# Routing and gathering the tokens of a mixture-of-experts layer tile by tile, and moving one gated product into the first group of experts

## The reference

```python
merged = sigmoid(ga) * (a @ w_br_a) + sigmoid(gb) * (o @ w_br_b)
x = layernorm(DN_ALPHA * x + merged @ w_out, ln1_g, ln1_b)
moe_out = hier_moe(x, w_rg, w_re, w1, w3, w2)
ple_term = sigmoid(x @ w_ple_gate) * (ple @ w_ple)
x = layernorm(DN_ALPHA * x + moe_out + ple_term, ln2_g, ln2_b)

def hier_moe(x, w_rg, w_re, w1, w3, w2):      # cut: shapes left out
    g_top, g_idx = top_k(softmax(x @ w_rg), 1)            # one of 4 groups
    e_logits = (x @ w_re) of that group                   # 8 experts in a group
    e_top, e_idx = top_k(softmax(e_logits), 2)            # two of them
    wts = g_top * e_top / e_top.sum()
    # each token goes to its two experts e: (silu(x @ w1[e]) * (x @ w3[e])) @ w2[e]
    # and the two results are added with the weights wts
```

## Time and profile before

| | us |
|---|---|
| median of 3 runs (lowest, highest) | 1733.82 (1733.11, 1735.64) |
| the profiled execution | 1733.89 |
| its span in the trace | 1732.1 |
| TensorE busy in it | 1411.0 (81%) |
| VectorE busy in it | 468.5 (27%) |
| ScalarE busy in it | 280.3 (16%) |

### The profile page before, as it was taken

How to read it: one execution, slowest core, us unless ns; L and a number is a source line. 1 busy time by engine, 2 the same in 40 slices (tenths; PEclk the granted TensorE clock), 3 DMA queues, 4 the chain that set the end, 5 groups by cost and what they waited for, 6 DMA issues and landing times.

```text
span 1732.1 us, 20248 instructions
## 1 busy us (share of the span) xinstructions
PE 1411.0 (81%) x8536; PEld 651.8 (38%) x8537; DVE 468.5 (27%) x1025; ACT 280.3 (16%) x677; POOL 49.5 (3%) x95
## 2 busy tenths in 40 slices
PE   5999999999977667766597999989999577667753
PEld 3556665553422212221254566645433122212211
DVE  3132563452211011100224415634512111011004
ACT  1322232111100000000125323230201000000001
POOL 1200000000000000000021000000000000000000
PEclk9999999999988878888798999999999888888887
DMA  8312413667999999999842024147499999999992
GB/s 281 106 47 98 152 50 114 230 283 295 426 427 426 427 427 426 427 425 427 346 151 74 1 98 152 49 141 297 190 404 426 427 427 427 427 426 426 427 427 102
DMA packets 97454, 490.98 MB, mean 283 GB/s; under 512 B 9264, under 2 KB 15184, under 8 KB 47696
## 3 DMA queue, kind: packets, MB, share of 16 engines
q1 hardware_dynamic: 92608, 478.16, 67.6%
q0 software_dynamic: 4752, 11.45, 2.0%
HBM read 486.69 MB, written 2.89 MB: 283 GB/s over the span
## 4 chain that ended last, share of the span: by engine, by line
PE 55%; DMA 29%; SPq 10%; DVE 3%; ACT 2%; issue 1%; DVEq 0%; POOL 0%; ACTq 0%
PE bank L862 52%; SPq L721 10%; DMA arena<-in_w_e_up 6%; DMA arena<-in_w_e_down 6%; DMA lb<-in_w_e_down 5%; DMA cst<-in_w_e_gate 3%; PE bank L900 2%; DMA xT<-in_w_e_gate 2%; DMA arena<-in_w_e_gate 2%; DMA cst<-in_w_e_up 2%; DMA lb<-in_w_e_gate 2%; DMA xT<-in_w_e_down 1%; DMA ring<-in_w_in 1%; DVE x_sb L1769 0%; DVE arena L1766 0%
## 5 line engine op out<-in xcount | busy, mean ns | idle before, releaser
L862 PE MATMUL bank<-ring,arena 128*32 128x512 f32 (+4 forms) x1720 | 458.0, 628 | 184.3 <-DMA arena<-in_w_e_up 41.1
L862 PE MATMUL bank<-arena 128*32 128x512 f32 (+11 forms) x2648 | 537.0, 540 | 68.1 <-DMA cst<-in_w_e_gate 22.2
L862 PE MATMUL bank<-ring,xT 128*32 128x128 f32 (+5 forms) x2496 | 451.8, 390 | 4.7 <-ACT xT L1436 2.3
L862 PEld LDWEIGHTS bank<-ring,arena 128*32 128x32 f32 (+1 forms) x1720 | 136.3, 135 | 460.6 <-issue 451.3
L862 PEld LDWEIGHTS bank<-ring,xT 128*32 128x32 f32 (+1 forms) x2496 | 218.0, 140 | 207.6 <-issue 189.5
L862 PEld LDWEIGHTS bank<-arena 128*32 128x32 f32 (+5 forms) x2648 | 203.8, 144 | 216.4 <-issue 211.1
L862 PE MATMUL bank<-cst,arena 128*32 128x512 f32 (+2 forms) x240 | 124.6, 659 | 1.7 <-ACT arena L1687 1.7
L862 PE MATMUL bank<-x_sb,arena 128*128 128x512 f32 (+1 forms) x192 | 95.7, 624 | 0.6 <-DVE arena L2192 0.6
L862 PE MATMUL bank<-lb,arena 128*32 128x512 f32 x160 | 91.2, 724 | 0.0
L2172 DVE TENSOR_TENSOR arena<-arena,bank 128x512 f32<-128x512 f32 x16 | 11.0, 688 | 272.7 <-PE bank L862 272.7
L862 PE MATMUL bank<-xT,arena 128*32 128x512 f32 x128 | 76.0, 750 | 0.0
(11 more groups left out here) (226 smaller groups left out, 894.3 us busy)
## 6 DMA issues: line engine op xcount, KB each, us to landing
arena<-in_w_e_gate SPq DMA_DIRECT2D x64, 1024.0 KB, 26.2
arena<-in_w_e_up SPq DMA_DIRECT2D x60, 1024.0 KB, 26.5
arena<-in_w_e_down SPq DMA_DIRECT2D x58, 1024.0 KB, 26.3
ring<-in_w_e_down SPq DMA_DIRECT2D x52, 1024.0 KB, 26.4
ring<-in_w_e_up SPq DMA_DIRECT2D x48, 1024.0 KB, 26.8
ring<-in_w_e_gate SPq DMA_DIRECT2D x44, 1024.0 KB, 26.6
ring<-in_w_in SPq DMA_DIRECT2D x32, 1024.0 KB, 9.5
ring<-in_w_out SPq DMA_DIRECT2D x8, 1024.0 KB, 7.2
```

The costliest lines, as they stand in the source:

```text
L862: return pe.matmul(out, lhsT, rhs, start=first, stop=last, skip_group_check=True)
```

## The change

- Ranks are counted in the order 2, 0, 1 and tile by tile (`rank`): those of tiles 2 and 0 while tile 1 is still being mixed. `tri` has 512 on its diagonal, so a routed token's rank comes out as 512 and more, and `places` (512 to 543) takes the role of the counting row. The two steps that turned ranks to positions are gone, and the selection compares with the bank itself (`place_tile`).
- `gather_first` multiplies `x` as the stationary side with `sel`, 128 columns at a time, and so writes the first quad's tokens already transposed, for tiles 2 and 0 before tile 1's transposes and for tile 1 after its ranks. `X0`, its copies and the eight transposes are gone.
- `route_tile` has fewer steps: the logits of the experts are masked straight from the bank by one `min`, and the second one-hot is added in one step.
- The statistics of the norm are taken for each half of `w_out`'s product when it is added. Tile 1 is normalised in halves, and its first transposes wait for the first half (`x_half`). `w_out`'s columns are put in the order of `x` on the host.
- `plain(0, 0)` moves from ahead of quad 0 to behind `Y` of quad 0, and the transposed choice `ST0` behind `plain(0, 1)`. The slots of `pg`'s first half are given out later in `expert_slots`.

TensorE before, in layer 0, from the product of half of tile 0's large gate matrix (`ring,xT`) to the first expert product. `arena,cst` are rank and count matmuls, `x_sb,arena` the gathers.

The diff, cut to its core:

```diff
+RANK0 = 512
...
-            (("wo", 0, 1), 6), (("rt", 2), 7), (("t1", 0, 0), 0), (("t1", 0, 1), 1), (("rt", 0), 3), (("wo", 1, 1), 2),
...
+            (("rt", 2), 7), (("t1", 0, 0), 0), (("t1", 0, 1), 1), (("wo", 0, 1), 6), (("rt", 0), 3),
...
-    j += [(("Y", 0), 5), (("Y", 1), 6)] + plain(1, 1, 1, 2) + plain(1, 2, 3, 4) + combine
+    j += [(("Y", 0), 5), (("Y", 1), 6)] + plain(0, 0, 7, 0) + plain(1, 1, 1, 2) + plain(1, 2, 3, 4) + combine
...
     first_g, first_y = 3, 7
-    turns += [(first_g + 1.5, i) for i in pg[0:2]] + [(first_y + 1.5, i) for i in [pl] + pg[2:4] + [XT_SLOT]]
+    turns += [(first_y + 1.2, i) for i in pg[0:2]] + [(first_y + 1.5, i) for i in [pl] + pg[2:4] + [XT_SLOT]]
 
...
-                    for h in range(2):
-                        job_read(pe, (layer, "t1", t, h))
                     b = open_bank((layer, "rt", t))
                     for c in range(8):
+                        if c % 4 == 0:
+                            job_read(pe, (layer, "t1", t, c // 4))
...
                     for h in range(2):
+                        if t == 1 and h == 0:
+                            pe.wait_ge(x_half, layer + 1)
+                        else:
+                            pe.wait_ge(ln_out, ln_place(2 * layer + 1, t))
                         transposes(layer, ("t1", t, h), [((c % 4) * P, P, x[0:NT[t], t, c * P:c * P + P]) for c in range(4 * h, 4 * h + 4)])
...
+                def rank(t):
+
+                    pe.wait_ge(route_out, 3 * layer + MIX_ORDER.index(t) + 1)
+                    b = open_bank((layer, "rk", t))
+                    for k, s in enumerate(MIX_ORDER[0:MIX_ORDER.index(t)]):
+                        mm(b[0:NT[t], 0:32], ones[0:NT[s], 0:NT[t]], route[0:NT[s], s, :], k == 0, False)
+                    done(mm(b[0:NT[t], 0:32], tri[0:NT[t], 0:NT[t]], route[0:NT[t], t, :], t == MIX_ORDER[0], True))
+
+                def gather_first(tiles):
+
+                    for h in range(2):
+                        key = (layer, "XT0", h)
+                        b = open_bank(key) if tiles[0] == MIX_ORDER[0] else bank(key)
+                        for t in tiles:
+                            for c in range(4):
+                                k = 4 * h + c
+                                ins = mm(b[:, c * P:(c + 1) * P], x[0:NT[t], t, k * P:k * P + P], sel[0:NT[t], t, :],
+                                         t == MIX_ORDER[0] and c == 0, t == MIX_ORDER[2])
+                        if tiles[-1] == MIX_ORDER[2]:
+                            done(ins)
+
                 turn_mixed(2)
-                mix(0, 1)
+                half_mix(0, 0)
                 pe.wait_ge(rows_in, 80 * (layer + 1))
                 router(2)
                 turn_mixed(0)
-                half_mix = lambda h: project_half(layer, ("wo", 1), 1, mT, [("wo", 1, 0), ("wo", 1, 1)], h)
-                half_mix(0)
+                half_mix(0, 1)
                 router(0)
-                half_mix(1)
+                half_mix(1, 0)
+                rank(2)
+                rank(0)
+                half_mix(1, 1)
+                pe.wait_ge(sel_early, layer + 1)
+                gather_first((2, 0))
+                turn_mixed(1)
+                router(1)
...
-                turn_mixed(1)
-                router(1)
-                half_gate = lambda h: project_half(layer, ("pg", 0), 0, xT, [("pg", 0, 0), ("pg", 0, 1)], h)
-                half_gate(0)
-
-                pe.wait_ge(route_out, 3 * (layer + 1))
-                for t in range(3):
-                    b = open_bank((layer, "rk", t))
-                    for s in range(t):
-                        mm(b[0:NT[t], 0:32], ones[:, 0:NT[t]], route[:, s, :], s == 0, False)
-                    done(mm(b[0:NT[t], 0:32], tri[0:NT[t], 0:NT[t]], route[0:NT[t], t, :], t == 0, True))
+                rank(1)
+                pe.wait_ge(sel_out, QUADS * layer + 1)
+                gather_first((1,))
                 b = open_bank((layer, "cnt"))
...
-                pe.wait_ge(sel_out, QUADS * layer + 1)
-                gather([(layer, "X0", h) for h in range(2)])
-                pe.wait_ge(selw_out, QUADS * layer + 1)
-                transpose_choice((layer, "ST0"))
-                turn_tokens([(layer, "X0", h) for h in range(2)], [(layer, "XT0", h) for h in range(2)])
...
                         plain(0, 1)
+                        pe.wait_ge(selw_out, QUADS * layer + 1)
+                        transpose_choice((layer, "ST0"))
...
+                        plain(0, 0)
                         plain(1, 1)
...
                 dve.bn_aggr(mvs[0:n, 2 * t:2 * t + 2], ln_st[0:n, :]).then_inc(ln_var, 1)
                 if at == 3 * k + 1:
                     dve.wait_ge(*((lnw_in, 32 * k) if k else (ln0_in, 32)))
                 dve.wait_ge(ln_var, at)
-                step(dve.scalar_tensor_tensor(src[0:n, :], src[0:n, :], mvs[0:n, 2 * t:2 * t + 1], lnw[0:n, 0, :],
-                                              ALU.subtract, ALU.mult))
+                parts = [slice(0, 512), slice(512, 1024)] if first_half else [slice(0, 1024)]
+                for cols in parts:
+                    ins = dve.scalar_tensor_tensor(src[0:n, cols], src[0:n, cols], mvs[0:n, 2 * t:2 * t + 1], lnw[0:n, 0, cols],
+                                                   ALU.subtract, ALU.mult)
+                step(ins)
                 dve.wait_ge(ln_rstd, at)
-                dve.scalar_tensor_tensor(x[0:n, t, :], src[0:n, :], ln_rs[0:n, t:t + 1], lnw[0:n, 1, :],
-                                         ALU.mult, ALU.add).then_inc(ln_out, 1)
+                for cols in parts:
+                    ins = dve.scalar_tensor_tensor(x[0:n, t, cols], src[0:n, cols], ln_rs[0:n, t:t + 1], lnw[0:n, 1, cols],
+                                                   ALU.mult, ALU.add)
+                    if first_half and cols.start == 0:
+                        ins.then_inc(first_half, 1)
+                ins.then_inc(ln_out, 1)
 
...
+                    job_read(dve, key)
+                    step(half_stats(t, x[:, t, :], j))
...
-                    dve.memset(lg[:, 4:8], -BIG)
-                    dve.tensor_copy(lg[:, 0:4], bank(key)[0:n, 0:4])
-                    emptied(dve.tensor_copy(lg[:, 8:40], bank(key)[0:n, 4:36]), key)
-                    job_read(dve, key)
+                    step(dve.tensor_copy(lg[:, 0:4], b[0:n, 0:4]))
...
-                    step(dve.tensor_scalar(r[:, 48:52], iota[0:n, 0:4], r[:, 16:17], None, ALU.is_equal))
-                    step(dve.tensor_scalar(r[:, 52:56], r[:, 48:52], BIG, -BIG, ALU.mult, ALU.add))
-                    e4 = lg[:, 8:40].rearrange("p (g e) -> p g e", g=GROUPS)
-                    step(dve.tensor_tensor(e4, e4, bcast(r[:, 48:52], 2, PER_GROUP), ALU.mult))
-                    step(dve.tensor_tensor(e4, e4, bcast(r[:, 52:56], 2, PER_GROUP), ALU.add))
+                    step(dve.tensor_scalar(r[:, 48:52], iota[0:n, 0:4], r[:, 16:17], 2 * BIG, ALU.is_equal, ALU.mult))
+                    emptied(dve.scalar_tensor_tensor(lg[:, 8:40].rearrange("p (g e) -> p g e", g=GROUPS), bcast(r[:, 48:52], 2, PER_GROUP),
+                                                     BIG, b[0:n, 4:36].rearrange("p (g e) -> p g e", g=GROUPS),
+                                                     ALU.subtract, ALU.min), key)
+                    job_read(dve, key)
...
+                    step(dve.tensor_scalar(oh[:, 0:32], iota[0:n, :], r[:, 40:41], None, ALU.is_equal))
+                    dve.scalar_tensor_tensor(route[0:n, t, :], iota[0:n, :], r[:, 41:42], oh[:, 0:32],
+                                             ALU.is_equal, ALU.add).then_inc(route_out, 1)
+                    dve.tensor_scalar(oh[:, 32:64], iota[0:n, :], r[:, 41:42], None, ALU.is_equal)
...
+                route_tile(2)
                 mixed(0, 1)
-                route_tile(2)
                 route_tile(0)
+                place_tile(2)
+                place_tile(0).then_inc(sel_early, 1)
                 mixed(1, 1)
-                norm_mixed(1)
+                normalize(1 + 2 * layer, 1, x[:, 1, :], x_half)
                 read_x("t1", layer, xT, (1,))
                 route_tile(1)
-                for t in range(3):
-                    ins = dve.memset(posm[0:NT[t], t, :], 0.0)
-                step(ins)
-                for t in range(3):
-                    n = NT[t]
-                    key = (layer, "rk", t)
-                    job_done(dve, key)
-                    emptied(dve.scalar_tensor_tensor(posm[0:n, t, 0:32], bank(key)[0:n, 0:32], 1.0, route[0:n, t, :], ALU.add, ALU.mult), key)
-                    job_read(dve, key)
-                    step(dve.tensor_scalar(posm[0:n, t, :], posm[0:n, t, :], -1.0, None, ALU.add))
+                place_tile(1).then_inc(sel_out, 1)
```

(10 more changed lines are left out.)

83 lines of the change are left out of this document (45 added, 38 removed), and 5 rows, old and new, of the table MIX_JOBS.

## The result

The changed kernel takes 1719.43 us (median of 4 runs, 1718.41 to 1720.66), beside 1733.46 for the kernel before on the same chip (4 runs): a ratio of 0.9923, with a 95% interval of 0.991 to 0.9935. It is faster by 14 us, where 22.8 were forecast. The profiled execution took 1719.57 (span 1717.8).

The account below looks back on a forecast made before the run. The expert weight stream bounds the kernel, so an earlier first expert product shortens it one for one: 1733.9 - 13.2 - 11.7 + 2.0 (stream losses) = 1711 us. Its own range was 1706 to 1716, the wide one 1705 to 1720.

Parts of the forecast that it names:

- rival A: Weight stream runs dry in quad 1, losing 3 to 5 us per layer, for 1715 to 1719; chance 0.20.
- the plateau's length: Each layer's stretch of full-rate weight streaming should stay 441 us within 2.
- the start moves 13.2 and 11.7 us: First expert product starts earlier by 13.2 us in layer 0 and 11.7 us in layer 1.
- the norm in halves: Tile 1's norm before its transposes: first half out at 374.5, whole row at 375.1; splitting adds two instructions of some 0.05.
- Cover and cost are within 0.2 of each other: Sixteen gather matmuls, 3.6 us together, just fit in TensorE's wait for tile 1's norm, all hidden.
- routing less 0.75: Tile 1's routing on VectorE, 3.34 us before, loses about 0.75 us of steps from its chain.
- ScalarE sits close: Ahead of the first expert product, table load (1.28) and sigmoid precede the token copy, ending at 384.0 against 384.2.
- the stream just survives: In quad 0, added TensorE work leaves the DMA queue 0.6 us to spare, against 10 before.
- 1.0 us a layer set aside: Allowance for loss in the weight stream because queues empty unevenly: 1.0 us per layer, bounds 0 and 5.
- Rival B: Clock or ScalarE ahead of the first expert product loses 1.7 us in each layer, giving 1714.5; chance 0.11.
- C: Low clock holds on into quad 0, costing 23 us more per layer, for 1757; chance 0.03.
- D: Something else, such as slots in later quads, holds the last landing, so time stays at 1733; chance 0.04.

Follow-up runs that it names:

- e12: The changed kernel with 128 unused bytes behind the constants on the core; 1709.82 us, ratio 0.9862.
- e13: e1 with 128 unused bytes behind the constants on the core; 1718.44 us, ratio 0.9912.
- e9: e1 with the sixteen gather matmuls of tiles 2 and 0 moved from under tile 1's norm to behind tile 1's routing; 1728.35 us, ratio 0.9974.
- e11: e1 with the former steps of `route_tile` for every tile; 1712.76 us, ratio 0.9884.
- e10: e1 with tile 1's row normalised whole and its transposes waiting for the whole row; 1710.67 us.
- e1: The changed kernel with `places` computed on the chip into unused columns, so later buffers lie where they lay before the change; 1705.99 us, ratio 0.9842.
- e6: e1 with 128 unused columns (512 bytes) behind the constants; 1706.0 us.
- m1: A separate kernel that only streams weights, all slots' start offset varied by phase; 422 GB/s at 0, 64, 256, 448, 427 to 428 at 128, 384.
- m2: The stream-only kernel of m1 with the number and order of well placed slots varied; from 422 GB/s (one in sixteen) to 428 (all at 384).

## Why the prediction was off, step by step

The time, 1719.43 us, lies above the forecast's own range (1706 to 1716). It is inside the wide range only by the place kept for rival A, which did not come; that is luck.

**Wrong: the plateau's length, "should stay 441 us within 2".** Its term took the stream's rate (426 GB/s) over from before. It became 421, which makes 5.4 us of each plateau (446.3 × (426.5/421 - 1) = 5.8 by the rates), 10.7 in all. The prediction weighed what the new constants compute and never what they push aside: 128 bytes put every slot on a slow start. Since e12 takes this away by a pad alone and e13 brings it back, the cause is shown. Why a start matters is not.

**Right, a little large: the start moves 13.2 and 11.7 us.** 12.5 and 10.9 came. Of the 0.75 short, 0.4 lie in the order laid out up to the last half of tile 1's product: from 350.93 to 369.30 it took 18.4, not 18.0. Another 0.2 are the gathers, priced at 0.224 each from the earlier trace rows; they took 4.41/16 = 0.276 and reached past the half row they were to hide under (without them, in e9, the transposes start 0.2 sooner). The rest, some 0.1, is the norm in halves, below. "Cover and cost are within 0.2 of each other" named this weak place.

**Right: routing less 0.75.** From 376.83 to 379.44, 2.61 instead of 3.34; undone in e11 it is 0.75 where the clock holds.

**Smaller than said: the norm in halves**, 0.26 of 0.6 (e10). Splitting a step cost 0.13 us and not 0.05, so the first half is out some 0.45 ahead of the whole row, and the gathers, which end later, leave half of that unused.

**Right: ScalarE sits close, and the table load costs 1.28.** Its copy ends 0.5 ahead of the product:

```profile
380.34 1.28 ACT L1694 ACT_TABLE_LOAD   x1
381.63 0.28 ACT L1694 ACTIVATE arena<-bank 128x128 f32<-128x128 f32 x1
382.04 0.59 ACT L1713 COPY arena<-bank 128x512 f32<-128x512 f32 x1
```

The sigmoid begins at the load's end again, and the load 0.02 us behind the exponential. The further drain of the Trainium skill (ScalarE: Activation LUTs, "What ACT_TABLE_LOAD costs") does not show here either.

**Right, with more to spare: the stream just survives (rival A falls).** First release to quad 1's first release is 459.14 - 386.87 = 72.27, forecast 73.3. The windows from 456 us on stay at 416 GB/s or more in the changed kernel, and 419 or more in e1 at the full rate. Of the 1.0 us a layer set aside nothing was used: at the full rate, in e1, the plateaus take 446.24 and 446.20 us, before 446.26 and 446.29. Without it the forecast would have been 1709.

**Rival B was real, but not in this kernel.** All six short waits of the changed kernel (0.23 to 0.38) left the clock at 1.00. e9 and e11 show how near it is: with the gathers out of the norm about 6 of the 10.3 us a layer go by the clock, and with a wait of 1.12 there are 1.6 more in one layer of two. Of the 12.5 us a layer that the change gains ahead of the first product, these gathers in another place would cost 10.3, and the prediction had counted their place as 3.6 us of cover only. **C and D** did not come.

With its buffers on a fast start the same change takes 1706 (e1, e6) to 1709.8 (e12), and the forecast without the unused 2 us, 1709, lies between: the mechanism of the gain was right, and what was missed stood in a line of constants. The 4 us between 1706 and 1710 are as much as runs of one kernel differ by, so that 1709 comes this close is worth no more than that.

## What to carry to other kernels

When a kernel streams weights for most of its time, a change's side effect on the addresses of its buffers is a term of the sum: compare where each slot begins before and after, and the GB/s in the plateau, not only the DMA share, which read 1.01 at either rate. A pad of 128 bytes is a cheap experiment, and was worth 10 us here, beside the 23 that the change gains ahead of the plateaus. Work put into TensorE's waits ahead of a critical stretch can pay more than its own time: here 16 matmuls of 4.4 us were worth 10.3 in each layer, because with them moved the clock fell as well (e9).

## What the runs showed of the hardware

- A stream of 1 MB pieces (128 partitions of 8 KB) into the core's memory reached 427 to 428 GB/s where slots begin 128 bytes above a multiple of 256, and 422 where they begin at 0, 64, 192, 256 or 448, counted from the buffer's start (m1, m2). Half of the slots well placed give 426 to 428. The Trainium skill (DMA: Bandwidth & Descriptors, "How a descriptor splits into AXI transactions") has a transaction that reads start at an address that is a multiple of 256. Were the writing side bound in the same way, a start 128 above should cost more, not less; the measurement says otherwise and decides.
- TensorE's granted clock stayed at 1.00 over all six short waits of the changed kernel (0.23 to 0.38 us). It fell to 0.50 behind waits of 1.12 and 0.38 in one layer and not in the other (e11), and within a wait of 3.99 in both (e9). In e9 it fell a second time in both layers, under a row of 24 gather matmuls, with no wait over 0.38 us since it had come back. So the length of the last wait alone does not tell whether it falls.
